# Mixture-of-experts decoder layer on one core: the expert loop written as pieces, with the shared expert's late work between them

## The reference, cut to what matters

```
h = layer_norm(ALPHA * x + merged @ w_out)
scores = sigmoid(h @ w_router);  idx = top_k(scores + b_router, 8)          # 128 experts
gate = sel / sum(sel) * 2.5
routed[tok] += (silu(xb @ w_e1[e]) * (xb @ w_e3[e])) @ w_e2[e] * gate       # for each expert e
shared = (silu(h @ w_s1) * (h @ w_s3)) @ w_s2
y = layer_norm(ALPHA * h + shared + routed)
```

## Time and profile before

| | |
|---|---|
| median of 3 runs | 1912.57 us (1909.36 to 1912.9) |
| profiled execution | 1911.07 us, span 1909.3 us, mean granted TensorE clock 0.993 |
| TensorE products / weight loads busy | 1839.5 us (96%) / 1190.5 us (62%) |
| VectorE / ScalarE / GpSimd busy | 613.3 us (32%) / 391.3 us (20%) / 365.4 us (19%) |
| HBM over the span | 517.37 MB read, 41.48 MB written |
| expert loop | 812 us to 1865 us |
| gate and up products, L1989 | x4096, 461.1 us busy |
| output products, L2015 | x1024, 247.9 us busy |
| silu, L2117 | x64, mean 385 ns, 451.7 us idle before it, all for TensorE |
| base added on VectorE, L2328 | x8, mean 688 ns |
| one-hot on VectorE, L2154 | mean 820 ns |

### The profile page before, as it was taken

The page is one execution under the profiler, slowest core; times in us unless marked ns, Lnnn a source line. Parts: engine busy times, 40 slices in busy tenths (PEclk is TensorE's granted clock), DMA queues, the critical chain, the costliest instruction groups (busy, mean ns, idle before and its releaser), DMA issues.

```text
span 1909.3 us, 34117 instructions
## 1 busy us (share of the span) xinstructions
PE 1839.5 (96%) x12864; PEld 1190.5 (62%) x12864; DVE 613.3 (32%) x1536; ACT 391.3 (20%) x908; POOL 365.4 (19%) x525
## 2 busy tenths in 40 slices
PE   8989999999999999989999999999999999999997
PEld 7856778998877874655566555555555555555552
DVE  0577756872243213612111212221221111111113
ACT  1104545541301002311111111111111111111113
POOL 1000002888881000001110111111111111111110
PEclk9999999999999999999999999999999999999999
DMA  5343212011323125589999999999999999999997
GB/s 162 118 167 111 89 34 52 3 39 67 139 83 117 67 69 218 212 322 417 411 397 374 404 419 406 389 382 420 420 420 420 420 421 420 421 420 420 421 415 252
DMA packets 110623, 523.20 MB, mean 274 GB/s; under 512 B 27278, under 2 KB 30606, under 8 KB 60118
## 3 DMA queue, kind: packets, MB, share of 16 engines
q1 hardware_dynamic: 84892, 482.54, 63.5%
q0 software_dynamic: 20544, 37.04, 5.3%
q10 hardware_dynamic: 5114, 2.62, 0.5%
HBM read 517.37 MB, written 41.48 MB: 293 GB/s over the span
## 4 chain that ended last, share of the span: by engine, by line
PE 64%; DMA 19%; POOLq 10%; issue 3%; DVE 1%; POOL 1%; SPq 1%; ACT 1%; DVEq 0%; ACTq 0%
PE bank L1989 18%; DMA arena<-in_w_e 16%; PE bank L2015 8%; PE bank L1343 5%; PE bank L491 5%; PE bank L1900 4%; PE bank L462 4%; POOLq L1044 4%; PE bank L1834 3%; PE bank L1931 3%; PE bank L1924 2%; PE bank L1350 2%; PE bank L1860 2%; PE bank L2002 1%; POOLq L1063 1%
## 5 line engine op out<-in xcount | busy, mean ns | idle before, releaser
L1989 PE MATMUL bank<-arena 128*64 128x256 f32 x4096 | 461.1, 381 | 22.3 <-DMA arena<-in_w_e 16.1
L1989 PEld LDWEIGHTS bank<-arena 128*64 128x64 f32 x4096 | 294.9, 137 | 202.3 <-issue 44.1
L2015 PE MATMUL bank<-arena 128*64 128x512 f32 x1024 | 247.9, 605 | 0.0
L2300 DVE TENSOR_TENSOR arena<-bank,arena 128x256 f32<-128x256 f32 x64 | 27.2, 425 | 559.4 <-ACT arena L2117 559.4
L1343 PE MATMUL bank<-arena 128*128 128x276 f32 x768 | 184.5, 399 | 0.0
L1804 POOL DMA_INDIRECT arena<-h_rows,index x66 | 66.9, 1014 | 567.8 <-PE bank L1931 533.5
L2015 PEld LDWEIGHTS bank<-arena 128*64 128x64 f32 x1024 | 62.1, 136 | 170.2 <-issue 73.1
L1343 PEld LDWEIGHTS bank<-arena 128*128 128x128 f32 x768 | 146.9, 192 | 33.0
L1900 PE MATMUL bank<-arena 128*128 128x512 f32 x264 | 141.5, 619 | 0.9 <-ACT arena L2121 0.9
L1820 POOL DMA_INDIRECT routed_rows<-arena,index x64 | 64.5, 1008 | 381.5 <-ACT arena L2121 366.9
L1108 PE MATMUL bank<-arena 64*64 64x64 f32 (+2 forms) x2816 | 116.2, 236 | 4.7 <-DVE arena L1206 1.7
(11 more groups left out here) (329 smaller groups left out, 1929.6 us busy)
## 6 DMA issues: line engine op xcount, KB each, us to landing
arena<-in_w_e SPq DMA_DIRECT2D x384, 1024.0 KB
arena<-in_w_in SPq DMA_DIRECT2D x50, 512.0 KB, 3.4
arena<-routed_rows SPq DMA_DIRECT2D x7, 1024.0 KB, 20.0
arena<-routed_rows SPq DMA_DIRECT2D x12, 512.0 KB, 12.4
arena<-in_w_mem_kv SPq DMA_DIRECT2D x4, 1024.0 KB, 8.5
arena<-in_cache_mem_k SPq DMA_DIRECT2D x8, 512.0 KB, 4.5
arena<-in_cache_mem_v SPq DMA_DIRECT2D x8, 512.0 KB, 5.7
arena<-in_w_out SPq DMA_DIRECT2D x2, 2048.0 KB, 12.9
```

Of the source, the lines that this page charges most:

```text
L1989: mm = pe.matmul(p_gu[t * S:(t + 1) * S, x * DE:(x + 1) * DE], xt[:, v, c, t * S:(t + 1) * S], w13[2 * v + t][:, x, c, :], start=(c == 0), ...
L2015: mm = pe.matmul(p_y[t * S:(t + 1) * S, :], hidT[:, j, t * S:(t + 1) * S], w2[2 * v + t][:, j, h * 512:(h + 1) * 512], start=(j == 0), sto ...
```

## The change

The loop over the pairs is no longer one loop with tests in it. It is a sequence of shorter loops, `pairs(r, first, end)`, with the extra work between them, behind one test on the round. On TensorE there are ten pieces (in turns of two pairs: 0-4, 4-8, 8-12, 12-16, 16-18, 18-20, 20-22, 22-24, 24-26, 26-32), on ScalarE five and on VectorE seven (in turns of four pairs). The late groups stand after pairs 7, 15, 23 and 31, tile 0's rows after pair 35 (both halves), the bases of tiles 1 to 4 after pairs 39, 43, 47 and 51 (both halves in a row, in banks 6 and 7). The residual loads stand after pair 31. VectorE's addresses, which depended on the turn, become fixed for the late groups. The work of a pair is the same on each engine.

```diff
         def base(t, h):
             n, cols = RES_ROWS[t], slice(t * P, (t + 1) * P)
-            pe.wait_ge(s_base, 17 + 2 * (t - SUMMED) + h)
+            pe.wait_ge(s_base, 17 + 2 * (t - SUMMED))
             for j in range(2):
-                mm = pe.matmul(m.ps[7][0:n, :], ...
+                mm = pe.matmul(m.ps[6 + h][0:n, :], ...
...
+        def pairs(r, first, end):
+            with pe.Fori(first, end) as i:
+                for v in range(2):
+                    pair(r, i, v)
...
         with pe.Fori(0, count) as r:
-            with pe.Fori(0, NP // 2) as i:
-                for v in range(2):
...
-                    with pe.If((NP // 2) * r + i < 13):
...
+            for g in range(4):
+                pairs(r, 4 * g, 4 * g + 4)
+                with pe.If(r < 1):
+                    shared_late(g)
+            pairs(r, 16, 18)
+            with pe.If(r < 1):
+                pe.wait_ge(sem("shared_down_loaded"), 16)
+                pe.wait_ge(s_base, 17)
+                for h in range(2):
+                    shared_rows(0, h)
+            for t in range(1, NTT):
+                pairs(r, 16 + 2 * t, 18 + 2 * t)
+                with pe.If(r < 1):
                     for h in range(2):
+                        base(t, h)
+            pairs(r, 26, NP // 2)
...
         with act.Fori(0, count) as r:
+            for g in range(4):
+                pairs(r, 2 * g, 2 * g + 2)
+                with act.If(r < 1):
+                    act.wait_ge(s_sh, 3 + g)
+                    act.activation(ssil[:, 0, :], m.ps[7][:, 0:THIRD], ACT.Silu).then_inc(s_ss, 1)
+                    if g == 3:
+                        act.wait_ge(s_sa, 6)
+                        for t in range(1, NTT - 1):
+                            act.dma_start(res[:, t, :], io["h_rows"][t * P:(t + 1) * P, :]).then_inc(s_res, 16)
...
+            pairs(r, 8, NP // 4)
...
         with dve.Fori(0, count) as r:
+            for g in range(4):
+                j, x = divmod(2 + g, 3)
+                pairs(r, 2 * g, 2 * g + 2)
+                with dve.If(r < 1):
+                    dve.wait_ge(s_ss, 3 + g)
+                    dve.tensor_tensor(sact[:, j, third(x)], m.ps[7][:, THIRD:2 * THIRD], ssil[:, 0, :], ALU.mult)\
+                       .then_inc(s_sa, 1)
+                    if g == 3:
+                        shared_samples()
+            pairs(r, 8, 9)
+            with dve.Fori(9, 9 + NTT - 1) as i:
                 for u in range(4):
+                    pair(r, i, u)
+                with dve.If(r < 1):
+                    dve.wait_ge(s_res, 16 * NTT - 16)
+                    for h in range(2):
+                        dve.wait_ge(s_bp, 2 * i + h + 1)
+                        rows = m.arena[:, ds(D * i + (O_RES - 8 * D + 512 * h), 512)]
+                        dve.scalar_tensor_tensor(out=rows, in0=rows, scalar=ALPHA, in1=m.ps[6 + h][:, :], op0=ALU.mult, op1=ALU.add)\
+                           .then_inc(s_base, 1)
+            pairs(r, 9 + NTT - 1, NP // 4)
```

More of the change, by code:

```diff
@@ new lines, in pairs, with pair @@
+        def pairs(r, first, end):
+            with pe.Fori(first, end) as i:
+                for v in range(2):
+                    pair(r, i, v)
+        def pair(r, i, v):
+            n = 2 * i + v
+            pe.wait_ge(s_xt, 2 * NP * r + 2 * n + 2)
+            for x in range(2):
+                pe.wait_ge(s_w1[v][x], (32 * NP // 2) * r + 32 * i + 32)
+                for c in range(KD):
+                    for t in range(2):
+                        mm = pe.matmul(p_gu[t * S:(t + 1) * S, x * DE:(x + 1) * DE], xt[:, v, c, t * S:(t + 1) * S],
+                                       w13[2 * v + t][:, x, c, :], start=(c == 0), stop=(c == KD - 1))
+                mm.then_inc((s_gate, s_gu)[x], 1)
+            pe.wait_ge(s_in[1 - v], (16 * NP // 2) * r + 16 * i + 16 * v + 16)
+            turn(1 - v, 0)
+            pe.wait_ge(s_hc, NP * r + n + 1)
+            find_slots(NP * r + n + AHEAD, n + AHEAD, v)
+            pe.wait_ge(s_xt, 2 * NP * r + 2 * n + 3)
+            turn(1 - v, 1)
+            pe.wait_ge(s_hid, NP * r + n + 1)
+            pe.wait_ge(s_idx, NP * r + n + AHEAD + 2)
+            for j in range(2):
+                mm = pe.transpose(p_ht[:, j * P:(j + 1) * P], hid[:, j::2], m.ident[:, :])
+            mm.then_inc(s_ht, 1)
+            pe.wait_ge(s_yv, NP * r + n + 1)
+            pe.wait_ge(s_ya, NP * r + n + 1)
+            spread_rows(1 - v, 0)
+            pe.wait_ge(s_w2[v], (32 * NP // 2) * r + 32 * i + 32)
+            pe.wait_ge(s_hc, NP * r + n + 2)
+            for h in range(2):
+                if h == 1:
+                    spread_rows(1 - v, 1)
+                    pe.wait_ge(s_yv, NP * r + n + 2)
+                for j in range(2):
+                    for t in range(2):
+                        mm = pe.matmul(p_y[t * S:(t + 1) * S, :], hidT[:, j, t * S:(t + 1) * S],
+                                       w2[2 * v + t][:, j, h * 512:(h + 1) * 512], start=(j == 0), stop=(j == 1))
+                mm.then_inc((s_y, s_y1)[h], 1)
@@ L2111, in scalar, with pairs @@
         count = rounds(act)
-        with act.Fori(0, count) as r:
-            with act.Fori(0, NP // 4) as i:
+        def pairs(r, first, end):
+            with act.Fori(first, end) as i:
                 for u in range(4):
@@ L2293, in vector @@
         count = rounds(dve)
-        with dve.Fori(0, count) as r:
-            with dve.Fori(0, NP // 4) as i:
-                for u in range(4):
[L2297 to L2329, removed]
@@ new lines, in pair @@
+        def pair(r, i, u):
+            n = 4 * i + u
+            one_hot(n + AHEAD, u % 2)
+            dve.wait_ge(s_sil, NP * r + n + 1)
+            dve.tensor_tensor(hid, p_gu[:, DE:2 * DE], sil, ALU.mult).then_inc(s_hid, 1)
+            dve.wait_ge(s_out[u % 2], (16 * NP // 2) * r + 32 * i + 16 * (u // 2) + 16)
+            slots_out(NP * r + n + AHEAD, (u + AHEAD) % 4)
+            dve.tensor_scalar(spread[:, u % 2].rearrange("p t n -> p (t n)"), token, found[:, u, 0:1], None, ALU.is_equal)
+            dve.wait_ge(s_ht, NP * r + n + 1)
+            dve.tensor_copy(hidT.rearrange("p j s -> p (j s)"), p_ht).then_inc(s_hc, 1)
+            dve.wait_ge(s_y, NP * r + n + 1)
+            dve.tensor_scalar(yg[:, u % 2, 0:512], p_y[:, :], found[:, u, 2:3], None, ALU.mult)\
+               .then_inc(s_yv, 1)
@@ new lines, in pairs @@
+        def pairs(r, first, end):
+            with dve.Fori(first, end) as i:
+                for u in range(4):
+                    pair(r, i, u)
+        with dve.Fori(0, count) as r:
+            for g in range(4):
[9 more added lines that the diff above has]
+            with dve.Fori(9, 9 + NTT - 1) as i:
+                for u in range(4):
+                    pair(r, i, u)
+                with dve.If(r < 1):
+                    dve.wait_ge(s_res, 16 * NTT - 16)
+                    for h in range(2):
+                        dve.wait_ge(s_bp, 2 * i + h + 1)
[3 more added lines that the diff above has]
+            pairs(r, 9 + NTT - 1, NP // 4)
```

65 lines of the change are left out of this document (5 added, 60 removed).

## The result

| | before | after |
|---|---|---|
| median of the runs | 1910.96 us (1904.66 to 1912.9, 4 runs) | 1889.13 us (1885.69 to 1891.93, 4 runs) |
| profiled execution, span | 1911.07 us, 1909.3 us | 1885.69 us, 1884.0 us |
| pair 0 begins | 811.98 us | 806.18 us |
| pair 0 to pair 63, first products | 1037.7 us | 1018.7 us |
| pair 63's first product to the end | 59.6 us | 59.1 us |

The ratio is 0.9901 (95%: 0.9874 to 0.9927), so the change is faster by about 1%, and the interval lies clear of 1. A second set of six runs beside 23 of the kernel before gave 0.9915 (0.9897 to 0.9933), 1890.92 against 1909.24 us, 18.3 us less.

The account below looks back on a forecast made before the run. The weight load queue was taken to bound the loop, run dry by bunched TensorE work; loop end 1865.4 - 1842.7 = 22.7 us gained, 1911.07 - 22.7 = 1888.4, so 1888 us, range 1882 to 1903.

Parts of the forecast that it names:

- the sum: Whole kernel: loop end moves from 1865.4 to 1842.7 us, a gain of 22.7 us, so 1911.07 becomes 1888.4.
- A pair costs the queue 16.27 us and TensorE 15.28, and the work in pairs 6 to 25 left the queue dry: Expert loop: 42 us of extra TensorE work within 20 pairs, 17.4 us a pair, is slower than the weight loads.
- The first turn's gap is a jump, and goes: Before pair 1: 4.61 us idle and a slow clock after jumping four untaken late groups; 7.3 us taken as gone.
- Rival C: First turn's gap stays, being a fetch of new code, not of a jump target; about 5 us, 1894; chance 0.15.
- TensorE's own line: Loop on TensorE if no load is late: 811.98 + 64 x 15.28 + 42.0 + 1, ending at 1832.9 us.
- The queue's line: Weight loads in the loop at 420 GB/s: last weights land at 1830.7 instead of 1853.4 us, loop ends at 1842.7.
- The lead is used up by pair 31: Weight loads start 19 us ahead; pairs eat about 1 us, late groups return 5.2; then the queue alone sets the pace.
- The tests: 4.8 us at most: Nested tests in TensorE's turns, pairs 2 to 27: removal gives 4.8 us at most, with 1 us kept for nine restarts.
- Nothing for the fall into new code: TensorE's ten loop pieces: falling into unfetched code taken as costing nothing, upper bound 7.3 us.
- rival A: First products after nine loop exits: each new piece stalls, 7.3 us each, 1944; chance 0.07, plus 0.03 for no change.
- B: the dips belong to the extra work: Rival, late groups: queue loses 18.4 us wherever they stand, only 4.3 us gained, 1907; half gives 1898; chance 0.13.
- The other engines' new waits cost nothing: ScalarE and VectorE behind late groups and base tiles: idle time covers the waits; without cover up to 1.4 us per tile.

Follow-up runs that it names:

- pieces_old_spots: Changed kernel's loop pieces without tests inside turns, but the extra work left at the old kernel's places; pair 0 to 63 1028.4 us, ratio 0.9965.
- little_extra: Changed kernel with most shared expert products left out, extra TensorE work from 42 us to about 12; pair 0 to 63 1018.8 us.
- tests_new_spots: Kernel before, one loop with nested tests, but the extra work at the changed kernel's places; pair 0 to 63 1034.4 us, ratio 1.0003.
- jump_twice_as_far: Changed kernel with a never-run block of eight late groups' products to jump over behind each of TensorE's ten pieces; pair 0 to 63 1074.3 us.
- half_w2: Changed kernel with one of the two w_e2 loads of a pair left out after the first two pairs; pair 0 to 63 1004.8 us.
- unrolled: Changed kernel with TensorE's pieces written out as 32 turns of straight code; pair 0 to 63 1018.1 us, ratio 0.9904.
- spread_to_35: Changed kernel with the extra work spread over pairs 3 to 35 only; pair 0 to 63 1021.7 us, ratio 0.9930.
- jump_behind_piece: Changed kernel with a never-run block of four late groups' products to jump over behind each of TensorE's ten pieces; pair 0 to 63 1020.6 us.

## Why the prediction was right

The time was 1889.1 us where 1888 was forecast, with the mechanism named; but part of that closeness is luck. The loop itself gained 19.0 us where the sum had 22.7. The forecast took the 22.7 off a profile whose loop begins at 811.98 us, and in the profile after it begins 5.8 us earlier by chance; in the second set of runs the medians differ by 18.3 us. By its steps:

- *A pair costs the queue 16.27 us and TensorE 15.28, and the work in pairs 6 to 25 left the queue dry.* Shown: the hole in GB/s is gone with the spread and stays without it (402 GB/s in pieces_old_spots), and 30 us of TensorE work less change nothing (little_extra).
- *The first turn's gap is a jump, and goes.* Shown: gone in the changed kernel, moved with the tests in tests_new_spots, and a gap like it (4.4 to 5.0 us with the slow clock behind it) made again by jump_twice_as_far. Rival C falls.
- *TensorE's own line, 1832.9 - 812.0 = 1020.9 us.* Measured 1020.2 by half_w2.
- *The queue's line.* Forecast: the last weights 1018.7 us after pair 0 begins; measured 1022.4. The term that was mis-sized is the rate: I took 420 GB/s throughout, and from 852.1 to 1828.5 us the loop moved 408.7 MB, 418.5 GB/s on average and 416 in the last stretch. Over these 976 us that is 3.4 us, nearly all of the 3.7 missing. Two other errors of the sum nearly cancel. It counted 1.0 MB that moves between 812.0 and 815.86 us, although its time starts at 815.86 (2.4 us too much). And from pair 0 to the last weights queue q1, which carries the weights and the loads of the routed rows, had moved 393.2 MB where it was 391.9 before (3.2 us too little); which of the two loads it was, the views don't tell.
- *The lead is used up by pair 31.* The first wait for weights came at pair 30. But then I had the queue alone set the pace; instead TensorE keeps its own 15.3 us from pair 36 to 55, since four pairs and a base tile (65 us) are just what the queue needs for four pairs.
- *The tests: 4.8 us at most.* Right for where they stood, and wrong as their worth. Stretched over the pairs of the spread they would cost some 20 us, with the first turn's gap and what else follows jumps 29.6, and eat the spread's gain whole (tests_new_spots). I priced the removal by the place it had before, and not by the place that the rest of the change gives it.
- *Nothing for the fall into new code.* Shown by unrolled and half_w2; rival A has its mechanism in jumps, not in falls, and there the price of 7.3 us each is about that of a far jump (6.2 to 9.8 us), while a near one cost nothing to 2.3.
- *B: the dips belong to the extra work.* Not so, 420 GB/s held past three late groups (852 to 1266 us). But spread_to_35 shows a small dip (407 to 410 GB/s in three slices) when groups follow each other every four pairs.
- *The other engines' new waits cost nothing.* No pair next to a late group shows more than the group's own 5.2 to 5.3 us until the lead is used up.

I ran no version that beats the changed kernel. With the weight queue at 418 to 420 GB/s and TensorE's line 14 us under it, a better one would have to move fewer bytes in the loop or shorten what stands before and after it. That wasn't tried.

## What to carry to other kernels

When two limits lie within a few per cent of each other, extra work in a loop is free only where the other limit has a lead to eat: spread it so that each stretch of the slower resource's buffer depth, with the work in it, stays at its pace. Put it between pieces of the loop and not behind tests in it, for tests that jump cost 0.2 us each on the engine's sequencer in every turn, and a longer spread multiplies them. Order code so that what runs first falls through: in these runs a jump over code that was not yet fetched left TensorE idle for anything from nothing to 10.6 us, and a fall into new code never did.

## What the runs showed that I had not expected

- Removing the tests, and the first turn's jump with them, gains 9.3 us of the loop by itself, spreading the work alone 3.3, and both together 19.0.
- The cost of a jump over unfetched code depends on how much it skips, on how often it hops and on what stands behind it: idle for up to 2.0 us over one block, and for nothing where a base tile follows; 4.4 to 5.0 us and the lower clock over twice that; 5.3 to 10.6 us when the same code is crossed in eight hops.
- A gap from such a jump can show up 20 to 40 instructions behind it, in the middle of straight code.
- An idle gap's length alone does not tell whether the granted clock falls. It stayed at 2.4 GHz behind the five gaps of 1.5 to 2.0 us in jump_behind_piece and behind those of 1.7 to 2.0 us in tests_new_spots, but behind one of 2.11 us in tests_new_spots TensorE went from 2.4 to 1.2 GHz for 3.4 us. In jump_behind_piece it did so at 811.5 us, behind idle gaps of 0.7 and 0.8 us that stand in the changed kernel too, where the clock stays up. With every gap of 4.4 us or more in the loops of these runs it fell.

```profile
1434.83 7.52 PE L1989 MATMUL bank<-arena 128*64 128x256 f32 x52 [2.11 <-issue]
...
1434.83:1438.50 3.67, 3.67 (x20) 2.25 (x22) 0.00 (x0) 0.00 (x0) 0.51 (x1) 0.55 1.02 426
```
